# Whole expert rows per transfer, three-pass projections and a fifth weight store in a two-block transformer kernel

## The reference, cut to what matters

```
x = x + mixer(rmsnorm(x))                # input projections; GLA heads and MoBA heads;
                                         # merged = sig(z_g)*(o_g @ w_proj_gla) + sig(z_m)*(o_m @ w_proj_moba); merged @ w_out
x = x + memory_attention(rmsnorm(x))     # w_cq, attention over 256 memory tokens, w_co
x = x + moe(rmsnorm(x))                  # 32 experts in 4 groups, 2 experts a token
    # each expert: hid = silu(x @ w_gate[e]) * (x @ w_up[e]);  y = hid @ w_down[e]
    # w_gate, w_up: 1024 x 512, w_down: 512 x 1024, float32: 2 MB (2.1e6 bytes) each
x = rmsnorm(x)
for layer in 2 layers:
    h = rmsnorm(x) @ w_in                # differential heads and stick-breaking heads, gates
    x = x + (g_diff*(o_diff @ w_o_diff) + g_sb*(o_sb @ w_o_sb)) @ w_out
    x = x + (silu(gate)*up) @ w_ffn_out  # w_ffn_in: 1024 x 5632, w_ffn_out: 2816 x 1024
out = rmsnorm(x)
```

## Time and profile before

| | |
|---|---|
| time, median of 3 runs | 1651.24 us (1647.64 to 1651.35) |
| profiled execution: time / span | 1651.45 us / 1649.6 us |
| busy: PE, DVE, ACT | 1445.2 us (88%), 733.6 us (44%), 549.2 us (33%) |
| granted TensorE clock, mean | 0.942 |
| first block up to the experts | 0 to 339 us |
| experts | 339 to 804 us |
| two layers, last norm, output | 808 us to the end |

### The profile page before, as it was taken

The page is one execution under the profiler, slowest core; times in us unless marked ns, Lnnn a source line. Parts: engine busy times, 40 slices in busy tenths (PEclk is TensorE's granted clock), DMA queues, the critical chain, the costliest instruction groups (busy, mean ns, idle before and its releaser), DMA issues.

```text
span 1649.6 us, 23166 instructions
## 1 busy us (share of the span) xinstructions
PE 1445.2 (88%) x10247; PEld 1186.3 (72%) x10247; DVE 733.6 (44%) x1068; ACT 549.2 (33%) x678; POOL 2.9 (0%) x8
## 2 busy tenths in 40 slices
PE   7998999997576676676799999999999999999998
PEld 6696888753232232232488888999988888899997
DVE  2545625421011011010487756666466674666642
ACT  2451522221001010010436734434343573443431
POOL 0000000000000000000000000000000000000000
PEclk9997999989889788898799999999999999999999
DMA  6552128379999999999734216555542422655540
GB/s 204 210 190 104 52 103 319 144 319 419 419 420 420 419 420 419 419 419 419 269 130 153 103 55 236 169 176 208 204 154 103 154 103 76 223 162 181 203 154 26
DMA packets 129805, 374.51 MB, mean 227 GB/s; under 512 B 9272, under 2 KB 54632, under 8 KB 105128
## 3 DMA queue, kind: packets, MB, share of 16 engines
q1 hardware_dynamic: 125735, 370.71, 59.0%
q0 software_dynamic: 528, 2.04, 0.4%
q10 hardware_dynamic: 3440, 0.25, 0.2%
HBM read 371.92 MB, written 1.06 MB: 226 GB/s over the span
## 4 chain that ended last, share of the span: by engine, by line
PE 66%; DMA 15%; DVE 8%; SPq 6%; ACT 3%; issue 2%; DVEq 0%; ACTq 0%
PE bank L597 33%; DMA ring<-in_w_exp_up 8%; PE bank L1142 7%; SPq L483 6%; DMA SZ<-in_w_exp_up 5%; PE bank L621 4%; PE bank L970 4%; DVE parts L1593 3%; PE bank L815 3%; PE bank L995 2%; PE bank L575 2%; PE bank L938 2%; PE bank L643 2%; DMA ring<-in_w_out 1%; ACT parts L1236 1%
## 5 line engine op out<-in xcount | busy, mean ns | idle before, releaser
L597 PE MATMUL bank<-hnr,parts 128*128 128x256 f32 x4032 | 495.5, 285 | 0.8 <-DVE parts L1593 0.8
L597 PEld LDWEIGHTS bank<-hnr,parts 128*128 128x128 f32 x4032 | 488.3, 193 | 6.1 <-issue 5.2
L1593 DVE TENSOR_TENSOR parts<-ring,parts 128x2048 fp32r<-128x2048 f32 x136 | 306.2, 2287 | 131.4 <-ACT parts L1236 129.8
L1236 ACT ACTIVATE parts<-ring 128x2048 fp32r<-128x2048 f32 x134 | 249.2, 1904 | 156.8 <-DMA ring<-in_w_out 60.1
L970 PE MATMUL bank<-ring,G 128*32 128x512 f32 x768 | 121.8, 793 | 86.8 <-DMA ring<-in_w_exp_up 86.1
L970 PEld LDWEIGHTS bank<-ring,G 128*32 128x32 f32 x768 | 30.8, 139 | 174.9 <-issue 114.3
L1924 DVE COPY SQ<-bank 64x512 f32<-64x512 f32 x16 | 16.8, 1048 | 308.0 <-PE bank L970 308.0
L597 PE MATMUL bank<-SKr,parts 128*128 128x256 f32 x960 | 123.9, 292 | 11.5 <-DVE SKr L1768 9.6
L597 PEld LDWEIGHTS bank<-SKr,parts 128*128 128x128 f32 x960 | 121.6, 200 | 13.9 <-issue 10.5
L1142 PE MATMUL bank<-Gr,parts 128*128 128x256 f32 x640 | 115.3, 283 | 0.0
L1371 ACT ACTIVATE SQ<-bank 64x512 f32<-64x512 f32 x16 | 16.8, 1052 | 275.9 <-PE bank L970 275.9
(11 more groups left out here) (313 smaller groups left out, 1389.4 us busy)
## 6 DMA issues: line engine op xcount, KB each, us to landing
ring<-in_w_in SPq DMA_DIRECT2D x60, 1024.0 KB, 7.3
ring<-in_w_exp_gate SPq DMA_DIRECT2D x48, 1024.0 KB, 25.9
ring<-in_w_exp_up SPq DMA_DIRECT2D x48, 1024.0 KB, 26.7
ring<-in_w_exp_down SPq DMA_DIRECT2D x48, 1024.0 KB, 26.2
ring<-in_w_ffn_in SPq DMA_DIRECT2D x44, 1024.0 KB, 7.7
ring<-in_w_ffn_out SPq DMA_DIRECT2D x20, 1024.0 KB, 6.0
hx<-in_w_exp_gate SPq DMA_DIRECT2D x16, 1024.0 KB, 25.4
SZ<-in_w_exp_up SPq DMA_DIRECT2D x16, 1024.0 KB, 26.7
```

Source lines behind the costliest of these rows:

```text
L597: m = mm(b(name)[:, T * half:T * half + T], part(chunk, ws)[:, k, P * mt:P * mt + P], src[xs][:, k, :], start=k == 0 and i == 0, stop=k == ...
L1236: A(parts[:, 2 * (r % 2), 2048 * i:2048 * i + 2048], ring[:, CHUNK[chunk][0], 2048 * i:2048 * i + 2048], ACT.Copy).then_inc(high_made, 1)
L1593: v.tensor_tensor(parts[:, 2 * (r % 2) + 1, at], ring[:, CHUNK[chunk][0], at], parts[:, 2 * (r % 2), at].bitcast(F32), ALU.subtract).then_ ...
```

## The change

- `fill` moves whole experts' matrices: a group of gate and up is now gate and up of one expert (two transfers of 2 MB, 16 KB a partition), and a group of down is the two experts' down matrices. The last down group is still four transfers.
- A fifth store: the store (ring 2, 3) is number 4, and store 1 is made of `G[:, 2048:6144]` and of `tail` and `hn`, now one allocation. `xe`, which was in `G`, goes to `TMP`. Groups use store g mod 5. The first five groups are issued in the order 4, 0, 2, the gate half of 1, 3, the up half of 1, at new places.
- `pair`: PE multiplies expert e of the pair as four side-by-side matmuls (gate, up) x (two halves of the contraction) in the same bank, ACT copies the bank for e = 0 and DVE for e = 1, each 128 partitions; PE waits for ACT's copy before e = 1, with `combine` and `turn_weights` between. The turn becomes 8 matmuls with a matrix `halves` that also adds the two halves. `combine` comes before `gather`.
- PE loads the count and branches ahead of the last pair; the last pair stands in both arms. SP asks for 44 used groups before it issues the second block.
- The projections join `SPLIT`: `high`/`low` for the weights, `first_highs`/`first_lows` for the first activations (`og`/`od`), `second_highs`/`second_lows` for the second ones, which replace DVE's copies out of PSUM. `second_lows` for bo0, bo1, bo2 stand at heads 2, 4, 6, behind that head's other work, not at 1, 3, 5. `head_apply` is at heads 4, 5, 5, 6.
- `merge` places `low` of the second projection and of `out0` between its products.

```diff
-SPLIT = [n for n in ALL_CHUNKS if not n.startswith(("ckv", "proj", "cq", "co"))]
+SPLIT = [n for n in ALL_CHUNKS if not n.startswith(("ckv", "cq", "co"))]
...
-        stores = ((ring[:, 2], ring[:, 3]), (ring[:, 4], ring[:, 5]), (ring[:, 0], ring[:, 1]), (hx[:, :], SZ[:, :]))
+        stores = ((ring[:, 4], ring[:, 5]), (G[:, 2048:6144], tail_hn[:, :]), (hx[:, :], SZ[:, :]), (ring[:, 0], ring[:, 1]),
+                  (ring[:, 2], ring[:, 3]))
...
+            def fill(pair, part_of, store, landed_sem, late_sem=None, slots=(0, 1)):
+                for j in slots:
+                    w = a["w_exp_down"][0][2 * pair + j] if part_of == 2 else (a["w_exp_gate"], a["w_exp_up"])[j][0][2 * pair + part_of]
+                    k = 4 if part_of == 2 else 8
+                    to, src = stores[store][j].rearrange("p (k n) -> p k n", k=k), w.rearrange("(p k) n -> p k n", p=P)
+                    if late_sem is None:
+                        sp.dma_start(to, src).then_inc(landed_sem, 16)
...
             used(sp, "out0")
+            fill(1, 1, 4, store_landed[4])
+            used(sp, "out1")
             fill(0, 0, 0, store_landed[0])
-            used(sp, "out1")
-            fill(0, 1, 1, store_landed[1])
-            fill(1, 0, 3, store_landed[3])
+            fill(0, 2, 2, store_landed[2])
+            full(sp, "co3")
+            fill(0, 1, 1, store_landed[1], slots=(0,))
             used(sp, "cq")
             used(sp, "co")
-            fill(0, 2, 2, store_landed[2])
+            fill(1, 0, 3, store_landed[3])
+            full(sp, "ht3")
+            fill(0, 1, 1, store_landed[1], slots=(1,))
+            for g in range(STORES, GROUPS - 1):
+                sp.wait_ge(m["used"], g - STORES + 1)
+                fill(g // 3, g % 3, g % STORES, store_landed[g % STORES])
...
-            sp.wait_ge(m["used"], GROUPS - 1)
+            sp.wait_ge(m["used"], GROUPS - 4)
...
# merge_out
+                                for i, (ws, xs) in enumerate(PASSES):
+                                    m = mm(b(name)[:, T * half:T * half + T], part(chunk, ws)[:, k, P * mt:P * mt + P],
+                                           src[xs][:, k, :], start=k == 0 and i == 0, stop=k == 3 and i == 2)
...
# pair, PE
+                for e in range(2):
+                    landed_of(e)
+                    if e:
+                        pe.wait_ge(s["gu_a"], n + 1)
                     for k in range(4):
                         for c in range(4):
+                            at = 4 * (c % 2) + k
+                            m = mm(ps[0][SLOTS * c:SLOTS * (c + 1), :], xe[:, at, SLOTS * e:SLOTS * (e + 1)],
+                                   stores[store_of(e)][c // 2][:, HALF * at:HALF * at + HALF], start=k == 0, stop=k == 3)
                     m.then_inc(s["used"], 1)
+                    if e == 0:
+                        if not first:
+                            pe.wait_ge(s["y_out"], n + 1)
+                            combine()
+                        turn_weights(s, n)
...
+                    for e in range(2):
+                        m = mm(ps[1][:, P * kk:P * kk + P].rearrange("p (u e i) -> p e u i", u=2, e=2)[:, e],
+                               gu[e][:, P * kk:P * kk + P], halves.rearrange("p (u i) -> p u i", u=2), start=True, stop=True)
...
+            for p in range(PAIRS - 1):
+                main_pair(p)
             pe.wait_ge(count_ready, 1)
             most = pe.value_load(cnt[0:1, 0:1], min_val=0, max_val=T)
             with pe.If(most > SLOTS):
+                last_pair()
...
+            with pe.Else():
+                last_pair()
...
# layers, ACT, loop over h
+                    if h in (2, 4, 6):
+                        second_highs(f"bo{h // 2 - 1}{x}", h // 2 - 1)
+                    if h == 7:
+                        first_highs(l + 1, od)
...
+                    if h in (5, 6):
+                        high("proj_diff" + x, [h - 5])
+                second_highs("bo3" + x, 3)
+                sigmoid("ga3" + x, z1)
+                high("proj_sb" + x)
+                sigmoid("gb3" + x, z2)
...
# layers, DVE, loop over h
-                    if h >= 4:
-                        last = head_apply(od, ["dn0" + x, "dn1" + x], h - 4, subs)
-                    if h == 7:
+                    for i in {4: (0,), 5: (1, 2), 6: (3,)}.get(h, ()):
+                        last = head_apply(od, ["dn0" + x, "dn1" + x], i, subs)
+                    if h == 6:
                         last.then_inc(og_ready, 1)
                     if h in (2, 3):
                         low("gb1" + x, [h - 2])
-                    if h % 2 == 1:
-                        name = f"bo{h // 2}{x}"
-                        full(dve, name)
-                        freed(v.tensor_copy(ob[:, h // 2, :], b(name)[:, 0:T]), name)
+                    if h in (2, 4, 6):
+                        second_lows(f"bo{h // 2 - 1}{x}", l + 1, h // 2 - 1)
+                    if h >= 6:
+                        low("proj_diff" + x, [h - 6])
+                first_lows(l + 1, od)
+                second_lows("bo3" + x, l + 1, 3)
```

More of the change, by code:

```diff
@@ L802, in _, with merge_out @@
                 moba_out(h)
-            def merge_out(sfx, chunks, o_first, wait_first, o_second, wait_second, n):
-                for chunk, o, names, wait in ((chunks[0], o_first, "pa", wait_first), (chunks[1], o_second, "pb", wait_second)):
-                    wait()
-                    landed(pe, chunk)
-                    w = tall[CHUNK[chunk][0]]
+            def merge_out(sfx, chunks, second, n):
+                for chunk, src, names in ((chunks[0] + sfx, first_parts, "pa"), (chunks[1] + sfx, second_parts, "pb")):
                     for j in range(4):
@@ L1300, in take_turned, with first_highs, second_highs @@
                 freed(A(probT[i % 2], b(name)[:, 0:384], ACT.Copy), name)
+            def first_highs(n, o):
+                act.wait_ge(og_ready, n + 1)
+                for i in range(2):
+                    A(two(first_parts[0], i), two(o, i), ACT.Copy).then_inc(first_high, 1)
+            def second_highs(name, i):
+                full(act, name)
+                A(second_parts[0][:, i, :], b(name)[:, 0:T], ACT.Copy).then_inc(second_high, 1)
             high("zg0")
@@ L1323, in _, with sigmoid @@
                     high("zm1", [h - 3])
[L1325 to L1330 removed]
+                if h == 5:
+                    high("proj_gla")
+                if h == 6:
+                    first_highs(0, og)
+            def sigmoid(name, z):
+                emptied(act, name)
+                A(z, z, ACT.Sigmoid).then_inc(z_sig, 1)
+            second_highs("mo3", 3)
+            sigmoid("zg3", z1)
+            high("proj_moba")
+            sigmoid("zm3", z2)
             high("out0")
@@ L1758, in _ @@
                     low("zm0" if h < 4 else "zm1", [h % 2])
-            full(dve, "mo3")
-            freed(v.tensor_copy(om[:, 3, :], b("mo3")[:, 0:T]), "mo3")
+            low("proj_gla")
+            first_lows(0, og)
+            second_lows("mo3", 0, 3)
             def xg_low(l, j):
@@ L1775, in merge @@
                         name = f"{names}{j}{x}"
+                        if names == "pb" and j == 0:
+                            low("out0" + x, [0])
                         full(dve, name)
                         freed(v.tensor_tensor(two(z, j), src_of(name, two(z, j)), two(z, j), ALU.mult), name)
+                        if names == "pa" and j < 2:
+                            low(("proj_sb" if x else "proj_moba") + x, [j])
                         if names == "pb":
@@ L1852, in _ @@
                     dve.wait_ge(sq_summed, j)
+            for u in range(2):
+                v.tensor_tensor(halves[:, SLOTS * u:SLOTS * u + SLOTS], ident[:, 2 * SLOTS * u:2 * SLOTS * u + SLOTS],
+                                ident[:, 2 * SLOTS * u + SLOTS:2 * SLOTS * u + 2 * SLOTS], ALU.add)
             v.memset(y, 0.0).then_inc(moe_sems[0]["y_out"], 1)
```

133 lines of the change are left out of this document (58 added, 75 removed).

## The result

The changed kernel takes 1622.0 us (median of 4, 1620.4 to 1623.9) against 1650.0 for the kernel before on the same chip: ratio 0.983, 95% interval 0.981 to 0.985. The profiled execution took 1622.9 us, its span is 1621.1. Against the profiled span of before, 1649.6, that is 28.5 us less. 1636.9 was predicted. The direction was right.

A forecast was written before the change was run, and what follows sets the result against it. Full transfer queues were taken to bound the experts' middle, and PE with what it waits for the rest. From 1651.45 us, -10.0 - 4.7 - 3.0 - 3.7 + 6.8 = -14.6 gave 1636.9, range 1623 to 1648.

The forecast's parts named there:

- Fifth store: Expert stage: 43 groups remain in the unbroken weight stream instead of 44, -10.0 us.
- Pieces of 16 KB: Expert weight stream: larger pieces cost less per byte, -4.7 us, the middle between a line's 9.4 and nothing.
- Work of a pair on PE: Expert stage: PE's extra turns and wait, perhaps 2.5 us a pair, are covered by transfer waits, 0.
- End of the experts: Last pair to next layer: loading the count earlier takes 4.19 us of issue off the path, -3.0 us.
- First block's projections: First block: 192 fast products replace 64 float32 ones, with fewer waits but later heads, -3.7 us, bounds -7 and 0.
- The three waits: First block, after the projections: PE's waits for DVE's split tiles shrink from 3.1 us to about 1, -2.0.
- The heads: First block's heads: DVE gives logits and next probabilities later by 1.2 and 1.0, PE has no slack, +2.2 us.
- Projections of the layers: Two layers: late bank reads delay the projections, 9.3 lost less 5.9 gained, +3.4 us each, +6.8 together.
- The first rival: Whole kernel: all of the line's 9.4 us comes and the banks cost half, -28.7, 1623 us; chance 0.17.
- The store alone: Rival: 16 KB pieces keep 420 GB/s and the banks cost 7 a layer, -2.7, 1649 us; chance 0.15.
- the slower banks: Rival for the layers: late bank reads start projections 18.4 us late, costing 12.5 more each, 1655 us; chance 0.06.
- PE as the bound: Rival for the experts: new PE work exceeds 7.5 us a pair and the stream gets holes, 1661 us; chance 0.02.

The follow-up runs named there:

- projections alone: The kernel before with only the three-pass projections and their new order added; four stores, 8 KB pieces and experts as before: 1638.3 us, ratio 0.993.
- count back: The changed kernel with the load of the count behind the last pair and the branch behind the last sum again: 1621.8 us, ratio 0.983.
- next weights late: The changed kernel, asking for the next block's first weights only when the last gate and up group is used: 1622.4 us, ratio 0.984.
- run 120: Not a kernel or experiment: "run" is a verb here, the text says that 192 products in a row take 120 ns each.
- `low` of `out0` behind: The changed kernel with both low halves of out0 behind the second merged tile again, in all three blocks: 1636.2 us, ratio 0.993.
- out0 held: The changed kernel, with the transfer of out0's weights waiting until the first block's gla projection is finished: 1632.3 us, ratio 0.989.
- old projections: The changed kernel with the whole projection part as in the kernel before; stores, pieces and the experts' pair stay changed: 1628.8 us, ratio 0.988.
- half the rows: The changed kernel with each store filled in 1 MB transfers cut across the partitions, 64 rows of 16 KB each: 1999.3 us.

## Why the prediction came out too slow

**Fifth store, -10.0.** Right: 9.9.

**Pieces of 16 KB, -4.7.** The rate rose as said, and the term was under-sized: 7.0. Taking the middle between a line and nothing was the choice that missed. Whether the length of the pieces or the number of transfers raised the rate is not shown. The estimate by the Trainium skill (DMA: Bandwidth & Descriptors, "Why small descriptors are slow"), 2.5, was further off; the trace disagrees with it in size (420 against 427 GB/s, 1.7%).

**Work of a pair on PE, 0.** Right. 79.8 us of waits for groups remain.

**End of the experts, -3.0.** The number came, 23.7 to 20.7 us from the last gate and up product to the layer, but by luck. The reason given was that the first product would follow ACT's last result by 5.4 us in place of 8.4. It follows by 8.0. The weights of the next block don't "land in time": they are split, and so ready for PE, 19.7 to 19.8 us behind the start of the last gate and up product, before (806.2) and after (777.3), and the moved issue only uncovers that. What became shorter is PE's tail up to ACT's last result, 15.3 to 12.7 us, at a granted clock of 1.00 (757 to 772) where it had been 0.71 (786 to 803). The projections alone have the same short tail (12.6 us) with the count where it was, and reach the layer after 21.2 us. So about 2.5 of the 3.0 us is the clock and 0.5 the edit, which is why neither count back nor next weights late lost anything.

**First block's projections, -3.7.** This is the step that failed. It measured about -10 (11.2 with the part undone, less 1.2 in the heads), or some -8 without what the edit does not explain, in either case beyond its own bound of -7.
- Products: 23.29 in place of 27.89, -4.6 and not -3.9. The 24.0 was scaled from a gate product of 48, where 192 in a row run 120 ns each.
- The sum has no term for the earlier release of the raw slot. The prediction read the wait of the first merged tile as DVE's order alone. Behind it stood the landing of `out0`'s weights, 8 us after the request that follows the gla projection's end. With the new order of `merge` and the weights held back, the wait is 6.2 us, and none of the 6.2 us gained ahead of `out0` is left.
- The three waits, "-2.0": with the weights there early, the order is worth 4.5, and most of it is clock. The sum priced a wait at its length, and the products behind it lose 1 to 2 us more.
- The heads, +2.2: measured +1 to +2.

**Projections of the layers, +6.8.** The delay was right: 9.3 predicted, 9.6 measured, with both named waits at their place and size. What stands against it was under-sized for the same reasons as in the first block: 7.0 and 8.9 us gained and not 5.9 each, so +3.3. The products give 4.6 of each there too, and the order 3.8 by the run with `low` of `out0` behind; whether the earlier release of the slot counts in the layers was not run.

Together the middle and the end gave 20.7 in place of 17.7, 3.0 more; everything up to the stream gave 11.3 in place of 3.7, 7.6 more; the layers cost 3.5 in place of 6.8. That is the 13.9 us between -14.6 and -28.5. The first rival (1623, "all of the line's 9.4 us, and the banks cost half") names nearly the time that came, but not what happened: the line's 9.4 was 7.0, and the banks cost all of their 4.6. The store alone is refuted by the run with pieces of 8 KB (7.0 us), the slower banks by the delay of 9.6 us and not 18.4, and PE as the bound by the 79.8 us that it still waits for groups.

What stays open: why the first experts' product ran at the lower clock in before and with out0 held, and at the full one in the other twelve profiles. Both have their `out0` products 29 us or more behind the projections, but so has old projections (30.8), which kept its clock. It is worth 3 to 4.5 us, and so 3 of the 11.7 us between before and changed are not explained by the edit. The clock of the tail at the end of the experts is as open, and worth 2.5 us. Together these are about 5.5 of the 28.5 us between the two profiles.

## What to carry to other kernels

When an operation is made to read a split copy, ask who was waiting for the raw buffer that it no longer holds: with that transfer late, the faster products and the new order together gained nothing here ahead of the next product. A new order has to fit what lands when: `low` of `out0` ahead of the second projection's tiles gained with early weights and stood in the way with late ones. In this kernel a wait of PE cost its length and 1 to 2 us more, since the products behind it ran at a lower clock for a while. When a gain has the predicted size, look whether the row that it was read from has moved: here 3.0 us were predicted and came, and the interval in question went from 8.4 to 8.0. A read that frees a bank belongs ahead of work with slack on the same engine: moving such reads, and the norms behind them, took another 21 us off, 19.5 of it in the layers' stages.

## What was not expected of the hardware

- A transfer to 64 partitions keeps all 16 engines busy (100.8%) and moves 225 GB/s, where one to 128 moves 427 (half the rows and changed).
- From pieces of 8 KB in transfers of 1 MB to pieces of 16 KB in transfers of 2 MB the rate rises by 1.7%, from 420 to 427 GB/s, in a queue that is full either way.
- Issues of transfers can block SP for long. The second half of the next block's first chunk took 16.5 us to issue while the queue was full; in the steady stream most issues of 2 MB take 0.33 to 0.43 us, the longest 2.2. SP's timeline of the changed kernel:

```profile
738.51 16.53 SPq L446 DMA_DIRECT2D ring<-in_w_in  x1
755.08 9.05 SPq L445 DMA_DIRECT2D ring<-in_w_in  x1
```
